# A 16-expert MoE step: three of an expert's 33 weight units have their lower part subtracted by GpSimd instead of VectorE

## What is computed

```python
def ec_moe(h, lp):
    probs = softmax(xf @ w_router)
    gate_vals, tok_idx = top_k(probs.T, cap)          # 64 latent + 16 context tokens for each expert
    xe = take(xf, tok_idx)
    hid = silu(einsum("ecd,edf->ecf", xe, w_e_gate)) * einsum("ecd,edf->ecf", xe, w_e_up)
    ye = einsum("ecf,efd->ecd", hid, w_e_down) * gate_vals[..., None]
    y = zeros_like(xf).at[tok_idx].add(ye)
```

## Time and profile before

| what | value |
|---|---|
| median of three runs | 2053.07 us |
| span of the profiled execution | 2054.4 us |
| PE busy | 1859.5 us (91%) |
| DVE busy | 1581.4 us (77%) |
| ACT busy | 1318.2 us (64%) |
| POOL busy | 164.9 us (8%) |
| moved by DMA | 624.65 MB, mean 304 GB/s |

### The profile page before, as it was taken

One profiled execution on the slowest core, in us unless ns is written; L12 is line 12 of the kernel. 1 busy time (PEld: TensorE's weight loads), 2 busy tenths in 40 slices (PEclk: granted clock), 3 DMA queues, 4 the chain that ended last, 5 costly groups with the idle time before them and its releaser, 6 DMA issues.

```text
span 2054.4 us, 33649 instructions
## 1 busy us (share of the span) xinstructions
PE 1859.5 (91%) x12843; PEld 1591.4 (77%) x12843; DVE 1581.4 (77%) x1387; ACT 1318.2 (64%) x1184; POOL 164.9 (8%) x95
## 2 busy tenths in 40 slices
PE   4898889659999999999999999999999999999995
PEld 3587767348788878788878888888888887878784
DVE  4432864568888888888888888888888888888885
ACT  5423651337777777777777767777777777777674
POOL 1000000010101010101010101010101010101100
PEclk8999999779999999999999999999999999999998
DMA  9232545459999999999999999999999999999993
GB/s 320 104 108 82 165 158 185 164 168 359 331 367 344 366 342 367 338 367 343 367 342 367 340 366 345 365 339 358 350 358 353 349 358 347 361 345 366 343 350 119
DMA packets 444766, 624.65 MB, mean 304 GB/s; under 512 B 12357, under 2 KB 373434, under 8 KB 444730
## 3 DMA queue, kind: packets, MB, share of 16 engines
q1 hardware_dynamic: 437434, 598.42, 86.4%
q0 software_dynamic: 6000, 21.01, 3.7%
q10 hardware_dynamic: 1296, 4.72, 0.6%
HBM read 608.65 MB, written 15.47 MB: 304 GB/s over the span
## 4 chain that ended last, share of the span: by engine, by line
PE 72%; DVE 13%; issue 7%; ACT 5%; DMA 2%; DVEq 0%; SPq 0%; POOL 0%; ACTq 0%; POOLq 0%
PE bank L1081 22%; PE bank L1083 22%; PE bank L1082 22%; DVE w_lo L998 6%; ACT w_hi L664 3%; DMA raw<-in_w_ada 2%; PE bank L1390 1%; DVE yrow L1055 1%; DVE w_lo L736 1%; DVE xem L1006 1%; ACT w_hi L496 1%; PE bank L1269 1%; DVE hid L1019 1%; PE bank L1372 0%; DMA xg<-xn_dram,idx_g 0%
## 5 line engine op out<-in xcount | busy, mean ns | idle before, releaser
L998 DVE TENSOR_TENSOR w_lo<-raw,w_hi 128x2048 fp32r<-128x2048 f32 x528 | 1204.8, 2291 | 203.1 <-ACT w_hi L664 191.3
L664 ACT CAST w_hi<-raw 128x2048 fp32r<-128x2048 f32 x528 | 1008.6, 1913 | 221.8 <-PE bank L1083 221.5
L1081 PE MATMUL bank<-w_hi,xe_hi 128*80 128x256 f32 x2816 | 795.6, 283 | 25.8 <-DVE w_lo L998 22.3
L1082 PE MATMUL bank<-w_lo,xe_hi 128*80 128x256 f32 x2816 | 787.4, 280 | 0.0
L1083 PE MATMUL bank<-w_hi,xe_lo 128*80 128x256 f32 x2816 | 784.1, 278 | 0.0
L1081 PEld LDWEIGHTS bank<-w_hi,xe_hi 128*80 128x80 f32 x2816 | 416.6, 148 | 46.6 <-ACT w_hi L664 18.3
L1082 PEld LDWEIGHTS bank<-w_lo,xe_hi 128*80 128x80 f32 x2816 | 417.6, 148 | 10.9
L1083 PEld LDWEIGHTS bank<-w_hi,xe_lo 128*80 128x80 f32 x2816 | 417.6, 148 | 0.0
L1081 PE MATMUL bank<-w_hi,hT_hi 128*80 128x512 f32 (+1 forms) x864 | 340.6, 394 | 21.2 <-DVE hT_lo L1023 21.2
L1083 PE MATMUL bank<-w_hi,hT_lo 128*80 128x512 f32 (+1 forms) x864 | 340.4, 394 | 0.0
L1082 PE MATMUL bank<-w_lo,hT_hi 128*80 128x512 f32 (+1 forms) x864 | 338.3, 392 | 0.0
(11 more groups left out here) (202 smaller groups left out, 1039.2 us busy)
## 6 DMA issues: line engine op xcount, KB each, us to landing
raw<-in_w_e_gate SPq DMA_DIRECT2D x176, 1024.0 KB, 7.9
raw<-in_w_e_up SPq DMA_DIRECT2D x176, 1024.0 KB, 7.9
raw<-in_w_e_down SPq DMA_DIRECT2D x176, 1024.0 KB, 7.7
raw<-in_w_ada SPq DMA_DIRECT2D x24, 1024.0 KB, 5.2
raw<-in_w_in SPq DMA_DIRECT2D x8, 1024.0 KB, 5.4
raw<-in_w_out SPq DMA_DIRECT2D x4, 1024.0 KB, 5.1
acc_sb<-acc_dram SPq DMA_DIRECT2D x5, 512.0 KB, 6.2
out<-acc_sb SPq DMA_DIRECT2D x5, 512.0 KB, 3.0
```

The lines of the kernel that those rows point to most:

```text
L664: nc.scalar.copy(w_hi[:, j % SPLIT, :], raw[:, j % RING, :]).then_inc(hi_done, 1)
L998: nc.vector.tensor_tensor(w_lo[:, j % SPLIT, :], raw[:, j % RING, :], w_hi[:, j % SPLIT, :], ALU.subtract).then_inc(lo_done, 1)
L1081: nc.tensor.matmul(out, xh, wh, start=first, stop=False)
L1082: nc.tensor.matmul(out, xh, wl, start=False, stop=False)
```

## The change

POOL now does the subtraction for units 10, 19 and 28 of each expert, with a semaphore `lo_pool` of its own. DVE leaves these three out. Whoever waited for `lo_done` to reach a unit (PE before multiplying, SP before reusing the ring slot) now waits for the semaphore and the count that `low_ready` gives for that unit. On POOL the three subtractions stand behind the index copies of the expert and ahead of the wait for `yrow`.

```diff
+POOL_UNITS = tuple(AT["down", g] for g in (2, 5, 8))
...
+        lo_pool = sem("lo_pool")
...
+        def low_ready(j, i):
+
+            e, j = divmod(j, EXP_UNITS)
+            by_pool = sum(q < j for q in POOL_UNITS)
+            if j in POOL_UNITS:
+                return lo_pool, by_pool + 1 + (i + e) * len(POOL_UNITS)
+            return lo_done, NPRE + j - by_pool + 1 + (i + e) * (EXP_UNITS - len(POOL_UNITS))
...
             with sp.Fori(1, EXPERTS) as i:
                 for j in range(EXP_UNITS):
-                    sp.wait_ge(lo_done, unit(j - RING, i) + 1)
+                    sp.wait_ge(*low_ready(j - RING, i))
                     expert_load(j, i)
...
                 pool.wait_ge(pool_step, 2 * i + steps0 + (1 if last else 2))
+                for j in POOL_UNITS:
+                    pool.wait_ge(hi_done, unit(j, i) + 1)
+                    nc.gpsimd.tensor_tensor(w_lo[:, j % SPLIT, :], raw[:, j % RING, :], w_hi[:, j % SPLIT, :], ALU.subtract).then_inc(lo_pool, 1)
                 pool.wait_ge(y_done, 2 * i + 4)
...
             def low_of(j, i):
+                if j in POOL_UNITS:
+                    return
                 dve.wait_ge(hi_done, unit(j, i) + 1)
...
-                pe.wait_ge(lo_done, unit(j, i) + 1)
+                pe.wait_ge(*low_ready(j, i))
```

More of the change, by code:

```diff
@@ L357, in _ @@
                 elif j >= RING:
-                    sp.wait_ge(lo_done, unit(j - RING, 0) + 1)
+                    sp.wait_ge(*low_ready(j - RING, 0))
                 expert_load(j, 0)
@@ L361, in _ @@
                 for j in range(EXP_UNITS):
-                    sp.wait_ge(lo_done, unit(j - RING, i) + 1)
+                    sp.wait_ge(*low_ready(j - RING, i))
                     expert_load(j, i)
-            sp.wait_ge(lo_done, unit(0, EXPERTS))
+            sp.wait_ge(*low_ready(EXP_UNITS - 1, EXPERTS - 1))
             sp.dma_start(fin_g[:, :], final_norm_g.unsqueeze(0).broadcast_to([P, D])).then_inc(fin_in, 16)
```

## The result

The changed kernel takes **2117.75 us** (median of four runs, 2116.85 to 2121.25) against 2053.64 us of the kernel before on the same chip: ratio 1.0316, 95% interval 1.0303 to 1.0328, 64.1 us slower. Forecast were 2102 us and slower, in a range of 2062 to 2150. The profiled execution took 2118.16 us, its span is 2116.4 us.

What follows compares the result with a forecast made beforehand. The prediction took PE to bound the kernel. DVE's relief gained 0 and POOL's lateness of 1.02 us at 3 x 16 units added 49 us to 2053.1, giving 2102 us, range 2062 to 2150.

Steps and rivals of the forecast that it cites:

- PE is the bound: PE is busy 1424.94 of 1491 us, ACT and DVE run at its pace; it waits for DVE 66 us.
- DVE's relief: Three DVE subtractions of 2.29 us fewer per expert, 110 us of DVE time in all, gain 0.
- The deadline: At units 10, 19 and 28 PE wants the lower part 3.62, 3.63 and 3.65 us after the upper part.
- POOL's length: POOL's subtraction at units 10, 19 and 28 takes 4.4 us, the middle of 3.5 and 5.2.
- Start and restart: POOL starts 0.1 us behind its wait; PE's matmul starts 0.15 us behind the lower part's end.
- The whole term: PE is late by 1.02 us at each of units 10, 19 and 28 in every expert, 49 us in all.
- DVE against POOL: Instructions with two SBUF inputs block each other; DVE's next unit stands behind POOL, costing nothing more.
- The mirror image: DVE's unit 11 stands still until POOL ends, as POOL's copies did behind DVE, with 0.4 us to spare.
- B: DVE breaks in on POOL's subtraction, or both share: lateness 3.3 to 5.6 us, 2213 to 2322 us; 6%.
- D: hT_lo is held up behind POOL's end as well: 18 us more, 2120 us; 4%.
- A: POOL makes the deadline at the three units, PE never waits, time stays at 2053 us; 9% with a gain included.
- C: POOL's instruction is longer than three passes; at 7 us PE is 3.6 us late, 2227 us; 5%.

Runs made afterwards that it cites:

- e4: The changed kernel with GpSimd subtracting only the first 1024 of 2048 columns of units 10, 19 and 28, the other half left out: 2062.66 us.
- e5: Only unit 25 on GpSimd, instead of units 10, 19 and 28 as in the changed kernel: 2093.8 us.
- e13: The changed kernel's semaphores and waits, but VectorE makes the subtractions of units 10, 19 and 28 and reports them on lo_pool: 2064.3 us.
- e9: The kernel before, nothing on GpSimd, with VectorE making the subtraction of units 10, 19 and 28 twice: 2115.19 us.
- e1: The changed kernel with only units 10 and 19 on GpSimd, VectorE doing unit 28 again: 2094.72 us.
- e2: The changed kernel with only unit 28 on GpSimd: 2085.96 us.
- e7: The changed kernel with VectorE forming hid of group 0 ahead of the lower part of unit 4 instead of behind it: 2091.53 us.
- e8: Only unit 4 of each expert on GpSimd, ahead of the wait for the scatter's landing, VectorE doing the others: 2039.11 us.

## Why the prediction was right, and where it was off

- **PE is the bound, DVE's relief is worth nothing.** Right, and shown: e4 takes the relief without the lateness, and an expert takes 99.74 us against 99.73.
- **The deadline.** Right: 3.62 us, and the stalls elsewhere stayed.
- **POOL's length.** Estimated 4.4 us from the memset rows, measured 4.60 (4588 to 4613 ns). The figure of the Trainium skill's page GPSIMD Engine Reference, section "Elementwise — side-by-side cycle accounting", 4497 ns, was nearer. Two reads in turn with the write hidden would have been 3.5 us and three streams in turn 5.2; the middle was a choice without a mechanism, so that it came within 0.2 us is luck. The 2.14 ns per element are 2.6 of the memset's 0.83, between two streams in turn and three.
- **Start and restart.** Taken 0.1 and 0.15 us, measured 0.08 and 0.06. The whole term: 1.02 forecast, 1.12 at the start of the unit and 1.15 by the expert's length, 49 against 55 us. The 0.03 us between may be the first matmul behind a wait (0.46 us instead of 0.39); that is not shown.
- **DVE against POOL.** The mirror image held: whoever comes second stands until the first has ended, and an instruction with one input in PSUM doesn't. Rivals B and D are out, and so are A (PE does wait for POOL) and C (4.60 us is under three passes, 5.2). That it costs nothing at units 11, 20 and 29 held as well (0.7 us to spare at 11). e5 shows how narrow that was: with another instruction in the same position it costs PE 1.1 us.
- **A missing term.** The falls of the clock, 9.4 us, a seventh of the loss. The forecast of 2102 us is 15.7 us short, 6 us for the late units and 9 us for this term, and the range held it only because it was made for the length of POOL's instruction. The prediction noted a granted clock of 1.00 and took it to stay. It costed the new waits on SP, POOL and ACT, but PE's at nothing and without a word; e13 shows that the separate semaphore alone, everything else equal, costs 10.5 us by way of the clock.

**What stays open.** Why PE restarts 0.09 us sooner with the changed waits. It waits on counts made from the loop's register, and before the change one count served for hi_done and lo_done alike. That this is the cause is argued, not shown, and it can't be all of it: PE started 0.10 us behind the unit's end at the late units of e9, which has the waits of before, and also behind POOL in e1 and e2, which have the changed ones. And that the longer idle stretch is what brings the falls is a correlation over fourteen traces: all seven with hid waited for 1.70 us on average have falls (2 to 12), none of the seven others (1.64 us in three, 0.5 us in four). e7 shows by one edit that shortening that wait removes them; that lengthening it alone, with PE's other waits untouched, brings them was not tried. Nor is an idle stretch always followed by a fall: in the changed kernel 6 of the 15 stretches of 1.7 us between 540 and 2031 us are, and in e5 2 of the 15 of 2.03 us at unit 25. The falls at an expert's start all begin 0.5 to 1.6 us behind PE's restart, in all seven traces. What decides which stretch is followed by one stays open.

## What to carry to other kernels

An instruction moved to an idle engine is bought at that engine's own length: put it against the time from its input's readiness to its user's demand (here 4.7 us against 3.6), unit by unit, and ask what moves up in the queue it left; only where something on the critical path stands behind it (unit 4, ahead of hid) is the relief worth anything. Then look whether a reordering gives the same without the second engine: here two reorderings on VectorE gave 30.7 us, the offload cost 64. And where the bound engine has idle stretches of a microsecond or two, read its granted clock piece by piece after every edit, even one that only changes what it waits on.

## What the runs showed of the hardware beyond the expected

- GpSimd's subtraction of two float32 tensors into fp32r takes 4.60 us for 128 x 2048 and 2.41 us for 128 x 1024; VectorE's takes 2.29 us for 128 x 2048.
- VectorE and GpSimd exclude each other in both orders when both have two inputs in SBUF: 2.29 became 3.67 us on VectorE behind GpSimd, and 0.89 became 4.59 us (the two shifts of e5 together); 4.60 became 5.13 us on GpSimd behind VectorE (e8).
- PE's granted clock fell to the 1.2 GHz level for 3.4 us behind an idle stretch of 1.71 us, in an expert in which PE was busy for 97.45 of 104.74 us, and this was worth 1.5 to 1.6 us each time.
- PE's first matmul came 0.15 us behind the end of VectorE's lower part in the kernel before and, at nearly all such places, 0.06 us behind it in e13, which changes only the semaphore.
